# The residual additions of a two-layer decoder step, issued by GpSimd where VectorE issued them

## The reference, cut to what matters

```python
def adaln_pre(x, m, g):
    return rmsnorm(x, g) * (1 + m[:, 1][:, None]) + m[:, 0][:, None]

def adaln_post(x, y, m, g, res_w):
    return x + res_w * m[:, 2][:, None] * rmsnorm(y, g)
...
h = adaln_pre(x, mod[:, 0], norm_pre[l, 0])
x = adaln_post(x, swiglu(h, ffn_w_in[l, 0], ffn_w_out[l, 0]), mod[:, 0], norm_post[l, 0], 0.5)
```

## Time and profile before

| | us |
|---|---|
| median of 3 executions | 2561.9 (2561.44 to 2562.82) |
| the profiled execution, its own time | 2561.68 |
| its span | 2559.8 |
| TensorE matmuls busy | 2469.6 (96%) |
| VectorE busy | 1207.4 (47%) |
| ScalarE busy | 1012.7 (40%) |
| GpSimd busy | 125.6 (5%) |

### The profile page before, as it was taken

How to read it: one execution, slowest core, us unless ns; L and a number is a source line. 1 busy time by engine, 2 the same in 40 slices (tenths; PEclk the granted TensorE clock), 3 DMA queues, 4 the chain that set the end, 5 groups by cost and what they waited for, 6 DMA issues and landing times.

```text
span 2559.8 us, 43978 instructions
## 1 busy us (share of the span) xinstructions
PE 2469.6 (96%) x18928; PEld 2199.5 (86%) x18928; DVE 1207.4 (47%) x1672; ACT 1012.7 (40%) x1414; POOL 125.6 (5%) x268
## 2 busy tenths in 40 slices
PE   5999999999989999999999999899999999999997
PEld 4999999865589999999999999776677899999997
DVE  3433346644456433356633246655554557633345
ACT  4322235527555322346522245432222446522243
POOL 0000000122200000000000000001222100000000
PEclk8999999999999999999999999999999999999999
DMA  6555245893535654665655345544444455553254
GB/s 257 173 153 154 80 159 170 257 237 110 165 98 166 205 152 139 200 224 171 188 174 157 111 160 181 164 151 148 158 156 165 136 151 176 176 149 93 89 173 144
DMA packets 118307, 413.96 MB, mean 162 GB/s; under 512 B 23258, under 2 KB 23386, under 8 KB 117730
## 3 DMA queue, kind: packets, MB, share of 16 engines
q1 hardware_dynamic: 82594, 289.47, 35.9%
q10 hardware_dynamic: 19584, 69.21, 8.6%
q0 software_dynamic: 15936, 52.47, 6.3%
HBM read 387.69 MB, written 23.41 MB: 161 GB/s over the span
## 4 chain that ended last, share of the span: by engine, by line
PE 82%; DVE 8%; ACT 5%; DMA 3%; issue 2%; SPq 0%; ACTq 0%; POOL 0%; POOLq 0%; DVEq 0%
PE PS L1790 65%; DVE WL L2025 3%; PE PS L1244 3%; PE PS L1750 3%; ACT WH L1874 2%; PE PS L1197 1%; PE PS L1192 1%; DMA AFIRST<-in_w_ada 1%; PE PS L1151 1%; DVE X L2092 1%; PE PS L663 1%; ACT Y L1918 1%; PE PS L1182 1%; DVE Y L2085 1%; PE PS L1163 1%
## 5 line engine op out<-in xcount | busy, mean ns | idle before, releaser
L2025 DVE TENSOR_TENSOR WL<-RAW,WH 128x1024 fp32r<-128x1024 f32 (+1 forms) x472 | 625.4, 1326 | 749.9 <-ACT WH L1874 749.8
L1790 PE MATMUL PS<-HH,WH 128*128 128x260 f32 x3584 | 845.7, 289 | 36.2 <-DVE HL L2112 15.0
L1790 PE MATMUL PS<-HH,WL 128*128 128x260 f32 x3584 | 824.4, 283 | 0.0
L1790 PE MATMUL PS<-HL,WH 128*128 128x260 f32 x3520 | 807.3, 283 | 0.0
L1874 ACT ACTIVATE WH<-RAW 128x1024 fp32r<-128x1024 f32 (+1 forms) x472 | 535.7, 1136 | 388.8 <-PE PS L1790 256.2
L1790 PEld LDWEIGHTS PS<-HH,WH 128*128 128x128 f32 x3584 | 595.9, 189 | 94.1 <-issue 79.0
L1790 PEld LDWEIGHTS PS<-HH,WL 128*128 128x128 f32 x3584 | 597.5, 189 | 0.0
L1790 PEld LDWEIGHTS PS<-HL,WH 128*128 128x128 f32 x3520 | 585.6, 189 | 0.7 <-issue 0.2
L1790 PE MATMUL PS<-GH,WH 128*128 128x260 f32 x1408 | 388.1, 286 | 2.4 <-DVE WL L2025 2.4
L1790 PE MATMUL PS<-GL,WH 128*128 128x260 f32 x1408 | 384.2, 283 | 0.0
L1790 PE MATMUL PS<-GH,WL 128*128 128x260 f32 x1408 | 383.6, 283 | 0.0
(11 more groups left out here) (302 smaller groups left out, 2202.1 us busy)
## 6 DMA issues: line engine op xcount, KB each, us to landing
RAW<-in_w_in SPq DMA_DIRECT2D x230, 512.0 KB, 3.6
RAW<-in_w_out SPq DMA_DIRECT2D x120, 704.0 KB, 4.1
AW<-in_w_ada ACTq DMA_DIRECT2D x128, 512.0 KB, 3.7
RAW<-in_w_odd SPq DMA_DIRECT2D x60, 512.0 KB, 3.6
RAW<-in_w_odout SPq DMA_DIRECT2D x30, 512.0 KB, 3.7
RAW<-in_w_even SPq DMA_DIRECT2D x28, 512.0 KB, 4.4
AFIRST<-in_w_ada SPq DMA_DIRECT2D x4, 2048.0 KB, 19.6
KV<-in_v_pages POOLq DMA_DIRECT2D x32, 256.0 KB, 3.7
```

The lines of the kernel that those rows point to most:

```text
L1790: last = nc.tensor.matmul(ps[:, x, 0:HT], w[:, k * P:(k + 1) * P], src[k0 + k][:, x, :], start=(begin and t == 0), stop=(end and t == 2))
L2025: nc.vector.tensor_tensor(low_, RAW[:, from_:from_ + w], high_.bitcast(F32), ALU.subtract).then_inc(lo_done, 1)
```

## The change

The two additions of every half boundary leave VectorE's program and stand in GpSimd's: first those of boundary 1, then `even_pool`, those of boundaries 2 to 4, `odd_pool`, those of 5 and 6, and then the four output transfers. Operands, waits and the signal `x_upd` are the same.

```diff
@@ in VectorE's program
-            def add_x(b, x, g):
-
-                dve.wait_ge(y_scaled[x], 2 * (b - 1) + g + 1)
-                part = X[:, 4 * g:4 * g + 4, x, :]
-                nc.vector.tensor_tensor(part, part, Y[:, 4 * g:4 * g + 4, x, :], ALU.add).then_inc(x_upd[x], 1)
...
                     if b and k == at_[f"scale{g}"]:
                         scale_y(b, x, g)
-                    if b and k == at_[f"add{g}"]:
-                        add_x(b, x, g)
@@ in GpSimd's program
+            def add_x(b, x):
+
+                for g in range(2):
+                    pool.wait_ge(y_scaled[x], 2 * (b - 1) + g + 1)
+                    part = X[:, 4 * g:4 * g + 4, x, :]
+                    nc.gpsimd.tensor_tensor(part, part, Y[:, 4 * g:4 * g + 4, x, :], ALU.add).then_inc(x_upd[x], 1)
+
...
+            add_x(1, 0)
+            add_x(1, 1)
             even_pool(pool)
+            for x, b in ((0, 2), (1, 2), (0, 3), (1, 3), (0, 4), (1, 4)):
+                add_x(b, x)
             odd_pool(pool)
+            for x, b in ((0, 5), (1, 5), (0, 6), (1, 6)):
+                add_x(b, x)
             for x in range(2):
                 for g in range(2):
                     pool.wait_ge(x_upd[x], 10 + g + 1)
```

## The result

The changed kernel takes 2586.52 us (median of 4 executions, 2583.27 to 2588.38) against 2562.36 for the kernel before (4 executions): +24.2 us, ratio 1.0096 [1.0084, 1.0108]. In a later comparison it took 2586.84 against 2561.49, +25.4 us, ratio 1.0100 [1.0085, 1.0114]. I had predicted 2589, with a range from 2567 to 2598. The profiled execution is the fastest of its four, 2583.27 us with a span of 2581.6, so sums made on its trace come out a few us short of the medians.

What follows compares the result with a forecast made beforehand. TensorE was taken to wait on the chain addition, squares, weight copy, split, matmul. Interior 21.7 plus end 6.3 gave 28.0 us on 2561.68, 2589.7, stated as 2589, range 2567 to 2598.

Steps and rivals of the forecast that it cites:

- the chain behind an addition: At half boundaries: addition, squares, weight copy, weight split, matmul have no slack; TensorE can get back 0.3 to 0.6 us.
- interior: The twenty additions of boundaries 1 to 5: 21.7 us slower in sum.
- place C: Four additions with nothing between scale and addition: signal 2.5 us after the scale, +1.2 each, +4.8 in sum.
- In turns, not side by side: Behind a split, GpSimd's addition waits for VectorE's whole split and starts at its end; forecast's chance 0.57.
- A: Ten additions with a 1024-column split after the scale: signal 3.64 us after the scale, +1.0 each, +10 in sum.
- B: Six additions with a 1408-column split after the scale: signal 4.04 us after the scale, +1.35 each, +6.9 counted.
- rival 1: All additions: GpSimd runs beside VectorE unhindered; interior +2.6, end +5.1, together +7.7 us, 2569; chance 0.30.
- the start as the sign to look for: GpSimd's additions start at the split's end if in turns, or 0.1 us behind the scale if side by side.
- The end, +6.3: Boundary 6: last addition 2.35 us later, four output transfers then under way at once, 8.0 us; +6.3 us.
- GpSimd's other work at nothing: Page transfers of `even_pool`, behind boundary 1's last addition: some 12 us later, costed at nothing; no deadlock or delay at `odd_pool`.
- Rival 2: All additions: a short, unhindered one of 1.7 us gives about +0.5 us, 2562; chance 0.05.
- rival 3: All additions: a long one of 3.3 us, in turns, gives +48 us, 2610; chance 0.08.

Runs made afterwards that it cites:

- late_sq_after: The changed kernel with ScalarE's squares one step later, behind the next weight copy, at 14 of 20 additions: 2570.85 us against 2561.49 for the kernel before.
- late_sq_before: The kernel before with ScalarE's squares one step later at the same 14 of 20 additions: 2555.02 us against 2561.49, ratio 0.9974.
- write_only: The changed kernel with GpSimd filling the part of X with ones in place of adding: 2551.86 us against 2560.90 for the kernel before.
- close_dve: The kernel before with every addition, still on VectorE, right behind its scale and ahead of the weight split: 2560.49 us against 2560.90.
- interior_only: The kernel before with only the additions of boundaries 1 to 5 on GpSimd, boundary 6 as before: 2580.09 us against 2561.33.
- after_again: The changed kernel once more, unaltered, in a later comparison: 2586.84 us, ratio 1.0100 to the kernel before.
- out_early: The changed kernel with each half's two output transfers right behind its two additions of boundary 6: 2586.51 us against 2561.33 for the kernel before.
- out_early_again: A repeat of out_early beside the unaltered changed kernel on one chip: 2589.07 us, ratio 1.0107 to the kernel before.
- tail_only: The kernel before with only boundary 6's additions on GpSimd and the four output transfers behind them: 2568.13 us against 2561.33.

## Why the prediction was right, point by point

- **What counts is the chain behind an addition.** Squares moved off it halve the interior's price, 18.6 to 9.0 us, with the additions' code untouched (`late_sq_after` against `late_sq_before`), and at the fourteen moved places it falls from 12.5 to 1.9 us in single traces. A signal up to 1.6 us earlier together with a VectorE that doesn't add gains 9.0 us (`write_only`); an earlier signal alone, paid for on VectorE, gains nothing (`close_dve`). In the changed kernel VectorE's freed time bought nothing that shows at boundary 3: its product for the gate is done at 1206.53, and ScalarE still waits for GpSimd until 1208.52.
- **2.4 us for an addition alone.** Measured 2.37 to 2.42, starting 0.08 behind the scale (I took 0.1). In place C the signal comes 2.46 to 2.50 us behind the scale, against the 2.5 predicted. By the estimate from the Trainium skill (GPSIMD Engine Reference, 3.1 Elementwise — side-by-side cycle accounting) it would have been 2.3; the trace is within 0.15 of it.
- **In turns, not side by side.** Right: behind a split the signal comes 3.43 us after the scale (A) and 3.82 (B), not 2.5 as rival 1 had it, and with `write_only` reading, not the engine, is shown to be what waits. The recorded start doesn't tell this: it stands 0.08 us behind the scale, as if nothing were in the way, and the wait is inside the recorded 3.35 and 3.73 us. I had named the start as the sign to look for; that was the wrong one, the end is right. By the same token a weight split of full length under the recorded addition, which I had said would refute the turns, doesn't: the split at 1204.97 lies there at its 1.22 us, and the signal's lateness shows who waited. Nor does GpSimd add at a slower pace under the split: behind splits that end 1.14 and 1.54 us after the scale its signals come 0.39 apart, as the splits' ends do (0.40). The other side of the rule shows too: GL, which comes while GpSimd holds on, takes 1.76 us for 0.43, and is done 0.3 behind the addition (1208.78 against 1208.49). At boundary 1 half 1 GpSimd came first, and it was the weight split that was held, as the timelines of VectorE and GpSimd after show:
```profile
461.56 1.24 DVE L2085 TENSOR_TENSOR Y<-Y,RS 128x1040 f32<-128x1040 f32 x1
463.11 3.28 DVE L2025 TENSOR_TENSOR WL<-RAW,WH 128x1024 fp32r<-128x1024 f32 x1 [0.30 <-ACT WH L1874]
462.88 2.42 POOL L2218 TENSOR_TENSOR X<-X,Y 128x1040 f32<-128x1040 f32 x1 [42.69 <-DVE Y L2085]
```
 These rows agree with the Trainium skill (SBUF — State Buffer, Who interferes with whom): two-input work of VectorE and reads of GpSimd exclude each other, writes don't take part, and who comes second waits. Held operations are also why VectorE's busy time fell by 15.0 us and not 29.6.
- **The size of the interior: a term too large.** I took the split's end, plus 0.1, plus 2.4: 3.64 in A and 4.04 in B. Measured 3.43 and 3.82, so 0.2 too much each: behind a split only 3.43 - 1.14 = 2.29 us pass, less than an addition alone. That GpSimd gets ready while it waits is my reading of this; no run tests it. And A wasn't one price, since I had taken the 2.62 us of one place for all ten signals before: they rise 2.29 us behind the scale at boundary 5 half 0, 2.96 at boundary 4 and 2.35 at boundary 1. So it was +0.81 us in six places, +1.15 in both of boundary 5 half 0, +0.46 at boundary 4, and +0.15 at boundary 1, where VectorE lost its turn. The twenty signals come 7.7 (A), 6.8 (B) and 4.8 us (C) later, 19.4 in sum; I had 10, 8.1 and 4.8, 22.9 in sum.
- **How much of it reaches TensorE.** I put 21.7 of my 22.9 on the path. The last variance starts 15.1 us later after (2561.89 against 2546.75) in single traces; `interior_only` gives +18.8 in medians, and the change less the end's 6.8 gives 17.4 and 18.6. So nine tenths or more of the 19.4 are exposed by the medians, and some eight tenths by the traces. TensorE's two rows of waits grew by 13.0 + 3.7 = 16.7, which covers the trace's 15.1. One term looks too large: I had priced the second additions of half 1 at boundaries 1 and 4 at the full 1.2 us each, and from there to the next scale the changed kernel falls behind by nothing in its trace and by 0.4 in sum in `after_again`. But `out_early` and `out_early_again`, the same code up to there, fall behind by 1.6 and 3.2 us there, so single traces don't settle this term.
- **The end, +6.3.** The number is right in part by luck. From the last variance to the span's end: 13.05 us before, 19.71 after, +6.7, and +6.8 by `tail_only`. Two errors cancel in it, 0.7 us too much for the additions and 1.0 too little for the transfers. Behind the second scale both additions took 4.57 us where I had 4.9, and the first transfer starts with the last addition's end and not 0.3 behind it, so it came 1.7 us later and not 2.35; from there to the span's end it took 10.05 us and not the 9.05 that I had taken from X coming in. The transfers landed in 5.0 us (median) in place of 4.0.
- **GpSimd's other work at nothing.** The first page transfer after starts at 474.17, 4.2 us behind the start of boundary 1's last addition, and in the waits of the changed kernel no engine waits for what they bring.
- **Rivals.** Rival 1 falls by the ends of the additions. Rival 2 needs an addition under 1.7 us and rival 3 one of 3.3: 2.4 excludes both. The sum was 28.0, the measured 24.2 and 25.4; the lateness that I had 3.5 us too large (the start-up inside the wait, and the two cheap places of half 1) makes up most of the difference.

## What to carry to other kernels

Before moving work from VectorE to an idle engine, look for who waits for it and what stands behind that waiter in its engine's order; that VectorE was busy for 47% of the time didn't tell the price. Here the same dependence could be taken off the path by moving the waiter, the squares, behind the next weight copy: that gave 17.5 us where moving the addition cost 24. And here GpSimd's addition didn't run beside VectorE's work when that too took both its operands from on-chip memory (SBUF): the addition waited (3.35 us for 2.4), or held VectorE's weight split up (3.28 us for 1.22).

## What the runs showed of the hardware that I had not expected

- GpSimd's addition of 1040 columns costs 2.40 us alone but adds only 2.29 behind an operation that it had to wait for, and its recorded start doesn't show the wait. The Trainium skill (Perfetto Trace Analysis, GPSIMD Engine Instruction) says to treat recorded spans of this engine as unreliable; here the ends hold, since ScalarE starts within 0.1 us of them.
- Four output transfers of 520 KB at the end, or two of them under the last matmuls, cost nearly the same: of what the early ones spare at the end (3.2 us) the weight blocks that come late take some 2.4.
- The granted clock in one stretch of 30 us was 0.83, 0.94 and 1.00 in three kernels that differ only in the step of their squares, and only from the second to the third did TensorE do more matmuls in it (129, 129, 168).
